# Inverse levels of blocks of 32 and 64 in a gated delta rule, on 32x32 and 64x64 corners of the TensorE array

## What is computed

```
decay = exp(where(tri_incl, gc[:, None] - gc[None, :], -inf))
A  = where(tri_strict, einsum('cd,sd->cs', k * beta, k) * decay, 0)
Tm = inverse of (A + I)          # lower triangular, unit diagonal
u  = Tm @ (v * beta)
w  = Tm @ (k * beta * exp(gc))
v_new = u - w @ S;  o = q_dec @ S + attn @ v_new;  S = S * g_last + k_tail^T @ v_new
```

## Time and profile before

| | |
|---|---|
| runs | 1267.7, 1267.64, 1267.85 us, median 1267.7 |
| profiled execution | span 1268.2 us from first to last instruction, 23324 instructions; no other time of this execution is given |
| TensorE busy | 1254.3 us (99%), 9041 matmul records |
| VectorE, ScalarE, GpSimd busy | 919.6 (73%), 699.2 (55%), 154.3 us (12%) |
| DMA | 212.83 MB, mean 168 GB/s |

### The profile page before, as it was taken

The page is one execution under the profiler, slowest core; times in us unless marked ns, Lnnn a source line. Parts: engine busy times, 40 slices in busy tenths (PEclk is TensorE's granted clock), DMA queues, the critical chain, the costliest instruction groups (busy, mean ns, idle before and its releaser), DMA issues.

```text
span 1268.2 us, 23324 instructions
## 1 busy us (share of the span) xinstructions
PE 1254.3 (99%) x9041; PEld 1169.6 (92%) x9041; DVE 919.6 (73%) x1290; ACT 699.2 (55%) x1082; POOL 154.3 (12%) x113
## 2 busy tenths in 40 slices
PE   9999999999999999999999999999999999999998
PEld 8997999999989998889998989999889998999986
DVE  6886874878778774447734547999758777999954
ACT  5556465654456343345354546666547567766642
POOL 0000142000000000000000001642200000464310
PEclk9999999999999999999999999999999999999999
DMA  7552332322355555555553444555564444454562
GB/s 300 189 173 101 133 134 101 133 68 68 152 197 188 195 179 185 198 170 182 183 209 109 156 173 167 198 169 195 194 221 171 162 154 163 167 188 175 197 224 93
DMA packets 30315, 212.83 MB, mean 168 GB/s; under 512 B 3488, under 2 KB 3616, under 8 KB 5152
## 3 DMA queue, kind: packets, MB, share of 16 engines
q1 hardware_dynamic: 29088, 206.53, 46.9%
q0 software_dynamic: 1152, 5.24, 1.1%
HBM read 210.71 MB, written 1.05 MB: 167 GB/s over the span
## 4 chain that ended last, share of the span: by engine, by line
PE 86%; DVE 8%; ACT 4%; DMA 1%; issue 1%; SPq 0%; DVEq 0%; ACTq 0%
PE lin L540 50%; PE lin L702 21%; DVE wlo L513 3%; PE lin L2883 2%; PE lin L567 2%; ACT whi L506 2%; PE lin L569 1%; DMA raw<-in_stream 1%; PE aux L2627 1%; PE aux L2599 1%; PE aux L2485 1%; ACT lm L1377 1%; PE aux L725 1%; PE aux L2745 1%; PE aux L2555 1%
## 5 line engine op out<-in xcount | busy, mean ns | idle before, releaser
L513 DVE TENSOR_TENSOR wlo<-raw,whi 128x2048 fp32r<-128x2048 f32 x183 | 427.4, 2338 | 170.8 <-ACT whi L506 170.1
L506 ACT CAST whi<-raw 128x2048 fp32r<-128x2048 f32 x192 | 365.3, 1906 | 179.5 <-DMA raw<-in_stream 147.0
L540 PE MATMUL lin<-xhi,whi 128*128 128x256 f32 (+2 forms) x1616 | 461.5, 286 | 1.0 <-DVE wlo L513 1.0
L540 PE MATMUL lin<-xlo,whi 128*128 128x256 f32 (+2 forms) x1616 | 457.0, 283 | 0.0
L540 PE MATMUL lin<-xhi,wlo 128*128 128x256 f32 (+2 forms) x1616 | 454.7, 281 | 0.0
L540 PEld LDWEIGHTS lin<-xhi,whi 128*128 128x128 f32 x1616 | 304.1, 188 | 3.0 <-DVE wlo L513 1.2
L540 PEld LDWEIGHTS lin<-xhi,wlo 128*128 128x128 f32 x1616 | 306.1, 189 | 0.0
L540 PEld LDWEIGHTS lin<-xlo,whi 128*128 128x128 f32 x1616 | 304.6, 189 | 0.4
L865 POOL TENSOR_TENSOR fu<-fs,ft 128x256 f32<-128x256 f32 x44 | 86.2, 1958 | 259.4 <-ACT fs L1479 259.4
L2292 DVE SCALAR_TENSOR_TENSOR ft<-fy,par,ft 128x254 f32<-128x254 f32 (+1 forms) x176 | 109.5, 661 | 5.9 <-DVE ft L2292 0.2
L540 PE MATMUL lin<-whi,xhi 128*128 128x256 f32 x256 | 74.2, 290 | 0.0
(11 more groups left out here) (454 smaller groups left out, 2123.2 us busy)
## 6 DMA issues: line engine op xcount, KB each, us to landing
raw<-in_stream SPq DMA_DIRECT2D x193, 1024.0 KB, 4.9
gp<-in_gains POOLq DMA_DIRECT2D x6, 512.0 KB, 3.9
c<-in_const SPq DMA_DIRECT2D x1, 1460.0 KB, 16.0
h<-in_x SPq DMA_DIRECT2D x2, 544.0 KB, 4.4
c<-in_const POOLq DMA_DIRECT2D x1, 1024.0 KB, 6.5
ht<-in_xtok POOLq DMA_DIRECT2D x1, 1024.0 KB, 9.6
out<-ht SPq DMA_DIRECT2D x1, 512.0 KB, 2.6
out<-ht SPq DMA_DIRECT2D x2, 256.0 KB, 2.0
```

The costliest lines, as they stand in the source:

```text
L506: nc.scalar.copy(whi[:, s0 % 4], raw[:, s0 % 4]).then_inc(hi_ready, 1)
L513: nc.vector.tensor_tensor(wlo[:, s0 % 4], raw[:, s0 % 4], whi[:, s0 % 4].bitcast(F32), ALU.subtract).then_inc(lo_ready, 1)
L540: ins = nc.tensor.matmul(out, a, b, start=start and n == 0, stop=stop and n == 2)
```

## The change

Levels 5 and 6 (blocks of 32 and 64) no longer work on full matrices; level 4 stays as it is. There is one mask left per group and chunk, the one of level 4, and the constant `levels` shrinks from 4 to 2 times 128 columns.

Level 5: for k = 0 and 1 (`lo = 64k`, `mid = 64k + 32`) the left product takes rows `lo:mid` of the unmasked triangle as 32x32 weights and the 32x32 block of the inverse as the moving operand, for all eight heads in a row, into partitions `mid:mid+32` of bank k. ScalarE copies it with the factor -1. The right product is again 32x32 with 32 columns. VectorE copies its result over the block of `tus` that is still zero. The two transposes of level 4's result come first, then both left groups, then both right groups, and the transposes of level 5 after both copies.

Level 6: per group of four heads the same with 64x64 weights and 64 columns, from partitions 0:64 into 64:128 and back, and the copy goes to the transposed places.

In VectorE's order `branch(0)` of chunk 2 moves ahead of level 5's copies, and the load of low parts stands between levels 5 and 6, as before. A wait of VectorE on its own masks (`al_ready`) ahead of `triangles(2, 0)` goes away.

```diff
-          ("levels", 4 * 128), ("cosa", T1), ("sina", T1), ("cosi", T1), ("sini", T1), ("turna", 128),
+          ("levels", 2 * 128), ("cosa", T1), ("sina", T1), ("cosi", T1), ("sini", T1), ("turna", 128),
...
 # ScalarE
-            def level(a, n):
+            def middle(a):
                 for g in range(2):
-                    if n > FIRST_LEVEL:
-                        turned_level(a, n - 1, g)
-                    left(a, n, g)
+                    turned_level(a, 4, g)
+                for k in range(2):
+                    b, mid = full(act, f"x{a}_5_{k}"), slice(64 * k + 32, 64 * k + 64)
+                    is_free(nc.scalar.activation(xss[a][mid, :, 0:32], wide(b[mid, 0:256], 32), ACT.Copy, scale=-1.0),
+                            f"x{a}_5_{k}")
+
+            def last(a, g):
+                b = full(act, f"x{a}_6_{g}")
+                is_free(nc.scalar.activation(xss[a][64:P, 4 * g:4 * g + 4, 0:64], wide(b[64:P, 0:256], 64), ACT.Copy,
+                                             scale=-1.0), f"x{a}_6_{g}")
...
 # VectorE
-            def mask_next(s, n):
-                for g in range(2):
-                    full(dve, f"x{s}_{n}_{g}")
-                    mask(s, g, n + 1)
...
+            def right_middle(s, k):
+                b, lo, mid = full(dve, f"y{s}_5_{k}"), 64 * k, 64 * k + 32
+                is_free(nc.vector.tensor_copy(tus[s][mid:mid + 32, :, 0:2, lo:mid],
+                                              b[mid:mid + 32, 0:256].rearrange("p (a b w) -> p a b w", b=2, w=32)),
+                        f"y{s}_5_{k}")
+
+            def right_last(s, g):
+                b = full(dve, f"y{s}_6_{g}")
+                is_free(nc.vector.tensor_copy(tus[s][0:64, 2 * g:2 * g + 2, 2:4, 64:P],
+                                              b[0:64, 0:256].rearrange("p (a b w) -> p a b w", b=2, w=64)),
+                        f"y{s}_6_{g}")
...
-            for n in range(FIRST_LEVEL, NLEVEL):
-                if n < NLEVEL - 1:
-                    mask_next(2, n)
-                else:
-                    branch(0)
-                    low_next()
-                right(2, n, 0)
-                right(2, n, 1)
+            for g in range(2):
+                right(2, g)
+            branch(0)
+            for k in range(2):
+                right_middle(2, k)
+            low_next()
+            for g in range(2):
+                right_last(2, g)
...
 # TensorE
+            def left_middle(a, k):
+                b, lo, mid = fill(f"x{a}_5_{k}"), 64 * k, 64 * k + 32
+                for p_ in range(8):
+                    ins = nc.tensor.matmul(b[mid:mid + 32, p_ * 32:p_ * 32 + 32], ats[a][lo:mid, p_, mid:mid + 32],
+                                           tus[a][lo:mid, p_ // 2, p_ % 2, lo:mid], start=True, stop=True)
+                is_full(ins, f"x{a}_5_{k}")
+
+            def right_middle(a, k):
+                after(pe, f"x{a}_5_{k}")
+                b, mid = fill(f"y{a}_5_{k}"), slice(64 * k + 32, 64 * k + 64)
+                for p_ in range(8):
+                    ins = nc.tensor.matmul(b[mid, p_ * 32:p_ * 32 + 32], tus[a][mid, p_ // 2, 2 + p_ % 2, mid],
+                                           xss[a][mid, p_, 0:32], start=True, stop=True)
+                is_full(ins, f"y{a}_5_{k}")
+
+            def left_last(a, g):
+                b = fill(f"x{a}_6_{g}")
+                for q in range(4):
+                    p_ = 4 * g + q
+                    ins = nc.tensor.matmul(b[64:P, q * 64:q * 64 + 64], ats[a][0:64, p_, 64:P],
+                                           tus[a][0:64, p_ // 2, p_ % 2, 0:64], start=True, stop=True)
+                is_full(ins, f"x{a}_6_{g}")
+
+            def right_last(a, g):
+                after(pe, f"x{a}_6_{g}")
+                b = fill(f"y{a}_6_{g}")
+                for q in range(4):
+                    p_ = 4 * g + q
+                    ins = nc.tensor.matmul(b[0:64, q * 64:q * 64 + 64], xss[a][64:P, p_, 0:64],
+                                           tus[a][64:P, p_ // 2, 2 + p_ % 2, 64:P], start=True, stop=True)
+                is_full(ins, f"y{a}_6_{g}")
...
+            def middle(a):
+                for g in range(2):
+                    turned_level(a, 4, g)
+                for k in range(2):
+                    left_middle(a, k)
+                for k in range(2):
+                    right_middle(a, k)
...
-            for n in range(FIRST_LEVEL, NLEVEL):
-                lefts(2, n)
-                right(2, n, 0)
-                right(2, n, 1)
+            lefts(2)
+            right(2, 4, 0)
+            right(2, 4, 1)
+            middle(2)
+            middle_turned(2)
+            for g in range(2):
+                left_last(2, g)
+            for g in range(2):
+                right_last(2, g)
             corrected(2, 0)
             corrected(2, 1)
```

More of the change, by code:

```diff
@@ L460, in program @@
         use_pair(0, "first_x2")
-        for n in range(FIRST_LEVEL, NLEVEL):
-            if n > FIRST_LEVEL:
+        for n in (4, 5, 6):
+            if n > 4:
                 use_pair(2, f"u2_{n - 1}")
@@ L1255, in act_gdn @@
             first_turned(1)
-            level(1, 4)
+            for g in range(2):
+                left(1, 4, g)
             b = full(act, "v0_0")
@@ L1262, in act_gdn @@
             nc.scalar.activation(gtmp[:, 2, 0, 1:2], eps[:, 0:1], ACT.Exp)
-            level(1, 5)
+            middle(1)
             turned_level(1, 5, 0)
@@ L1267, in act_gdn @@
             decay_maps(act, 2, 1)
-            left(1, 6, 0)
-            left(1, 6, 1)
+            last(1, 0)
+            last(1, 1)
             load_hi(s + 3, 0)
@@ L1284, in act_gdn @@
             first_turned(2)
-            for n in range(FIRST_LEVEL, NLEVEL):
-                level(2, n)
+            for g in range(2):
+                left(2, 4, g)
+            middle(2)
+            for g in range(2):
+                turned_level(2, 5, g)
+            for g in range(2):
+                last(2, g)
             nc.scalar.activation(gtmp[:, 2, 0, 1:2], eps[:, 0:1], ACT.Sqrt)
@@ L1945, in decayed_queries, with right @@
                 nc.vector.tensor_tensor(q, q, eg[:], ALU.mult).then_inc(S("ke"), 1)
[L1947 to L1951, removed]
+            def right(s, g):
+                b = full(dve, f"y{s}_4_{g}")
+                t = tus[s][:, 2 * g:2 * g + 2, 0:2]
+                is_free(nc.vector.tensor_tensor(t, four(b[:]), t, ALU.add), f"y{s}_4_{g}")
+            def right_middle(s, k):
[8 more added lines that the diff above has]
+                        f"y{s}_6_{g}")
             def residual(s, g):
@@ L2017, in dve_gdn @@
             first_level(1)
-            mask(1, 0, 4)
-            mask(1, 1, 4)
+            mask(1, 0)
+            mask(1, 1)
             low_next()
             low_next()
-            mask_next(1, 4)
-            right(1, 4, 0)
-            right(1, 4, 1)
+            right(1, 0)
+            right(1, 1)
             for g in range(2):
@@ L2035, in dve_gdn @@
             residual(1, 1)
[L2036 to L2038 removed]
+            right_last(1, 0)
+            right_last(1, 1)
             triangles(2, 0)
@@ L2619, in right, with lefts @@
+            def lefts(a):
+                for g in range(2):
+                    after(pe, f"first_x{a}_{g}")
+                    masked(a, g)
+                    left(a, 4, g)
+            def middle(a):
+                for g in range(2):
+                    turned_level(a, 4, g)
+                for k in range(2):
+                    left_middle(a, k)
+                for k in range(2):
+                    right_middle(a, k)
             def right(a, n, g):
@@ L2690, in pe_gdn @@
             read_state(1, 1)
-            masked(1, 6, 1)
-            left(1, 6, 0)
-            left(1, 6, 1)
-            right(1, 6, 0)
-            right(1, 6, 1)
+            left_last(1, 0)
+            left_last(1, 1)
+            right_last(1, 0)
+            right_last(1, 1)
             pe_products(pe, "kk", 2, 0)
@@ L3009, in constants @@
     lev.append(-((i[:, None] < i[None, :]) & same16).astype(f))
-    for n in range(FIRST_LEVEL, NLEVEL):
-        b = 1 << n
-        col = i[None, :] // b
-        lev.append(-((col % 2 == 1) & (i[:, None] // b == col - 1)).astype(f))
+    col = i[None, :] // BLOCK
+    lev.append(-((col % 2 == 1) & (i[:, None] // BLOCK == col - 1)).astype(f))
     c["levels"] = np.concatenate(lev, 1)
```

49 lines of the change are left out of this document (18 added, 31 removed).

## The result

Seven runs of the changed kernel have a median of 1270.7 us (1269.0 to 1272.9), seven of the kernel before on the same chip 1267.7: ratio 1.0023, 95% interval 1.0013 to 1.0034. The forecast was 1265.4, its range 1264.6 to 1269.2. The profiled execution took 1269.8, with a span of 1268.0.

What follows compares the result with a forecast made beforehand. TensorE, busy 1254.3 of 1268.2 us, was taken to bound the kernel. Gains of 1.3 us in chunk 2 and 1.0 in chunk 1 summed to 2.3, giving 1265.4 us on the median, range 1264.6 to 1269.2.

Steps and rivals of the forecast that it cites:

- The masks: VectorE, levels 32 and 64: dropping eight masks of 0.69 us is worth 0, since TensorE never waited for one.
- Thirty-two pairs of 32x32: TensorE, level 32: weight load and stream of a small matmul taken as 0.035 us, ends 0.031 and 0.111.
- Copies of 256 columns: Hand-overs in the levels: a 256-column copy taken as 0.37 us on ScalarE and 0.42 on VectorE.
- Level 32 in chunk 2: Gives nothing: products shrink from 3.6 to 2.2 us, but three waits and a tile-shape switch take the rest.
- Level 64 at the full clock: Level 64 in chunk 2 gains 1.3 us, with sixteen left and sixteen right pairs of 64 columns.
- Chunk 1 from its transposes to the products: Chunk 1 gains 1.0 us; a 1.2 us wait for ScalarE's eg hides what is saved before it.
- The waits: TensorE: about 0.5 us before level 16's second transposes, 0.6 before level 32's result's transposes; the 1.2 us ScalarE wait stays.
- rival (a): Levels 32 and 64: granted clock falls to 0.50, 1.7 us each; once 1267.1, twice 1268.8; 25% for one or two.
- a sparser stretch passed: Argument against a clock fall: the stretch at 271.5 to 274.9, busy 2.19 us, kept the clock at 1.00.
- (b): Levels 32 and 64: small pairs have a larger floor, 0.045 to 0.062 us, giving 1266.3 to 1268.7; 17%.
- (c): Level 32: price per instruction, not column; at 0.074 or more over 2.5 us slower, up to 1276.1; 13% in all.
- The 62 ns for each MATMUL: Skill's sequencer decode time: small pair would be 0.062 us, a loss of 1.0 us; set aside for 0.03 us loads.

Runs made afterwards that it cites:

- run 9: Changed kernel with linear-branch products moved between the small groups of chunk 1 alone: 1266.73 us, ratio 0.9990 to the kernel before.
- run 7: Changed kernel with linear-branch products moved between the small groups of both chunks: 1265.3 us, ratio 0.9978 to the kernel before.
- run 3: Changed kernel with unused full-size fp32r matmuls in its waits (3, 4, 9 in chunk 1; 2, 4, 0 in chunk 2): 1268.52 us, ratio 1.0000.
- run 6: Kernel before, with its full matrices, masks and adds, put in the changed kernel's order of levels 32 and 64: 1271.2 us, ratio 1.0026.
- Run 11: As run 7, with less fill in chunk 2, taken from the branch's second part, and VectorE's last branch product earlier: 1263.88 us, ratio 0.9969.
- run 4: Changed kernel with 128x128 weights and 32 moving columns at level 32, waiting for both copies at once: 1289.7 us, ratio 1.0164.
- run 5: Changed kernel with 32x32 weights but 128 moving columns at level 32, so another inverse is computed: 1283.1 us, ratio 1.0124.
- run 12: As run 3, with 6, 6, 12 unused matmuls in chunk 1 and 6, 6, 6 in chunk 2: 1266.63 us, ratio 0.9994.

## Why the prediction was wrong

**What held.** The masks were worth nothing: no wait of TensorE names one before or after. Thirty-two pairs of 32x32 take 1.09 us, 0.034 each with the last one's tail (taken: 0.035). Copies of 256 columns take 0.38 us on ScalarE and 0.42 on VectorE (taken: 0.37 and 0.42). At 64x64 eight pairs take 0.68 and sixteen 1.14, so 0.46 / 8 = 0.058, as taken. Level 32 in chunk 2 takes 313.31 - 308.98 = 4.33 us against 4.56 before (forecast 4.53). Level 64 at the full clock takes 313.73 - 310.30 = 3.43 (run 9), forecast 3.35, before 4.60. Chunk 1 from its transposes to the products takes 8.54, forecast 8.46. The waits stand where they were put: 0.6 us before level 32's transposes, 1.1 us behind eg; before level 16's second transposes 0.35 us in chunk 1 and 0.23 in chunk 2, expected 0.5 and 0.45. So the terms of the sum held. Taking the measured price of the falls off the profiled run gives 1269.8 - 1.63 (3.52 us from 276.24 to 279.76, in run 7 1.89 for the same sixteen) - 2.66 = 1265.5, where 1265.4 was forecast. One reading of the prediction was wrong without harm to this: it takes the span of 1268.2 and the median of 1267.7 for nearly the same. Wherever both are on record, an execution's time is 1.7 to 1.9 us over its span, so the profiled execution of before took an estimated 1270.0, 2.3 over the median, and its fall at 122.5 is most of that. The sum used rows from 262 on alone, where its clock was 1.00.

**What failed is rival (a), in its chance and in its size.** It had 25%, for one or two falls of 3.4 us, 1.7 us each and 1268.8 at the worst. Measured: both places fell in the profiled run, the second for 6.8 us, and together they cost 1.63 + 2.66 = 4.3. 4.3 lost against 2.3 gained is 2.0 slower, and the profiled run is 2.1 over the median of before. The median of seven is 0.9 higher still: the other runs have mean clocks down to 0.991, against 0.995 in the profiled one, which points to more or longer falls that no profile shows. The step at fault is the sentence "against: a sparser stretch passed". It measured sparseness by busy time: 2.19 of 3.40 us at 271.5 kept the clock, and that was counted against a fall. Runs 3 and 6 show that busy time does not order the falls: one came behind 3.34 us busy with 32x32 matmuls, none behind 2.59 busy with full-size ones. A small matmul's record counts as busy in the profile however little of the array it feeds. The row at 122.5, which stood behind small and 64-row work, was the nearer case. It could not have given the chance either: thirteen other profiles run the same code there without a fall. A single profile shows one draw. But all seven runs of the changed kernel have a mean clock of 0.995 or less, so 25% was far too low.

The Trainium skill (TensorE: Matmul & The Clock Gate, "What's actually happening") says that the gate is set by how busy the engine has been recently, and its passage "HAM oscillation" names idle gaps of TensorE as what brings the fall. Run 11's trace goes with it, in one execution: 0.50 right behind an idle gap of 1.84 us, a shorter gap than those of the passage. For the small matmuls the rule is too narrow: run 4 was busy, by its records, for 3.24 of 3.50 us and fell to 0.50.

Of the others, (b) and (c) are refuted by the pair at 0.034 or less. (By the prediction's own formula the lower end of (b) is 1266.6, not 1266.3; nothing hangs on it.) The 62 ns for each MATMUL that the Trainium skill (TensorE: Matmul & The Clock Gate, "Decode and dispatch") states for decode in the sequencer did not show up: the small pairs follow each other every 0.034 us.

**Open.** How little full-size work between small groups is enough was not measured finely: 3, 4 and 9 were too few in most runs, 6, 6 and 12 enough in most. Why one execution falls and the next of the same kernel doesn't, no profile here shows. How much of chunk 1's fall in the changed kernel is owed to the small matmuls and how much to the waits of 1.1, 0.36 and 0.25 us among them was not separated. That the seven slower runs of run 9 fell at chunk 2 is inferred from their mean clock alone.

## What to carry to other kernels

When a change turns full-size matmuls into small ones, price two things: the time of the pairs, and the granted clock of the next microseconds, which can cost more than the pairs save. Don't leave small groups in a row: put dense work that is due anyway between them, and look which engine's chain the dense work was covering before. Read the clock by stretches of a few microseconds and over several runs: the row in tenths and a single profile hide a loss that is 4 us in one run and 0 in the next. Before two spans are compared, see where the clock fell in each of the two traces.

## What the runs showed that had not been expected

- A busy TensorE can fall to 0.50: 3.34 of 3.40 us busy with 32x32 pairs (run 3), 3.24 of 3.50 with 128x128 weights and 32 columns (run 4), 3.40 of 3.40 with 32x32 weights and 128 columns (run 5).
- The kernel before has such a fall too, from 122.5 to 125.9, in one of the fourteen profiles that run this code; it makes that execution some 1.5 us longer.
- An idle filler can pay: 5 us of unused products took about 4 us off (run 12).
- Two kernels with the same code at a place differ by 2.66 us there through the clock alone (run 9 and the changed kernel, chunk 2).
- With the clock out of play, each of ten runs lay within 0.8 us (run 7); with it, twelve runs of one kernel spread over 5.7 us (run 3).
